# Gate norms of a streaming encoder layer: the sums as a row from one product with ones, and the row's powers on GpSimd in four pieces

## The reference, cut to what matters

```python
def rmsnorm(x, g):
    x32 = x.astype(jnp.float32)
    y = x32 * lax.rsqrt(jnp.mean(x32 * x32, axis=-1, keepdims=True) + EPS)
    return (y * g.astype(jnp.float32)).astype(x.dtype)
...
    h = h + mix @ w_out
    gate = jax.nn.sigmoid((rmsnorm(h, g_ple) @ w_pg).astype(jnp.float32))
    h = h + (gate * (p_i @ w_ple).astype(jnp.float32)).astype(h.dtype)
```

## Time and profile before

| | us |
|---|---|
| three timed runs: median (lowest to highest) | 2471.99 (2470.08 to 2472.39) |
| the profiled execution's own time | 2471.64 |
| its span, first to last instruction | 2469.8 |

### The profile page before, as it was taken

One profiled execution on the slowest core, in us unless ns is written; L12 is line 12 of the kernel. 1 busy time (PEld: TensorE's weight loads), 2 busy tenths in 40 slices (PEclk: granted clock), 3 DMA queues, 4 the chain that ended last, 5 costly groups with the idle time before them and its releaser, 6 DMA issues.

```text
span 2469.8 us, 27263 instructions
## 1 busy us (share of the span) xinstructions
PE 2446.9 (99%) x11188; PEld 2012.1 (81%) x11188; DVE 1036.0 (42%) x1584; ACT 641.5 (26%) x1005; POOL 217.7 (9%) x329
## 2 busy tenths in 40 slices
PE   9999999999999999999999999999999999999997
PEld 7888888888887888888888788888888888888886
DVE  5443343443445234444543433434434542344444
ACT  6221221221232223322432122122122232232223
POOL 1101101101101000000010110110110100000001
PEclk9999999999999999999999999999999999999998
DMA  6343243343243333223242432432432433322322
GB/s 213 107 127 117 83 122 116 88 121 118 87 121 120 99 98 107 70 79 114 80 150 85 134 107 81 138 107 77 139 111 77 129 117 118 110 72 86 94 68 103
DMA packets 180396, 264.84 MB, mean 107 GB/s; under 512 B 16720, under 2 KB 128656, under 8 KB 178992
## 3 DMA queue, kind: packets, MB, share of 16 engines
q1 hardware_dynamic: 143040, 171.87, 23.0%
q0 software_dynamic: 23376, 77.79, 9.8%
q10 hardware_dynamic: 13856, 13.44, 2.3%
HBM read 226.02 MB, written 37.02 MB: 106 GB/s over the span
## 4 chain that ended last, share of the span: by engine, by line
PE 97%; DVE 2%; DMA 0%; issue 0%; ACT 0%; POOL 0%; DVEq 0%; SPq 0%; ACTq 0%; POOLq 0%
PE acc L1360 88%; PE side L1360 8%; PE osb L1586 1%; PE side L1436 0%; PE side L1549 0%; PE side L1489 0%; DMA raw<-in_w_in 0%; DVE st L1071 0%; DVE Sp L1087 0%; DVE Ss L1095 0%; DVE HT L1340 0%; DMA Z<-in_x_t 0%; PE osb L1360 0%; DVE Z L1250 0%; DVE HT L1239 0%
## 5 line engine op out<-in xcount | busy, mean ns | idle before, releaser
L1360 PE MATMUL acc<-Ahi,Whi 128*128 128x512 f32 x2048 | 812.0, 396 | 7.2 <-DVE Alo L850 4.0
L1360 PE MATMUL acc<-Alo,Whi 128*128 128x512 f32 x2048 | 799.1, 390 | 0.0
L1360 PE MATMUL acc<-Ahi,Wlo 128*128 128x512 f32 x2048 | 798.9, 390 | 0.0
L485 ACT ACTIVATE Whi<-raw 128x1024 fp32r<-128x1024 f32 x319 | 337.9, 1059 | 1479.0 <-PE acc L1360 1465.7
L846 DVE TENSOR_TENSOR Wlo<-raw,Whi 128x1024 fp32r<-128x1024 f32 x319 | 390.8, 1225 | 733.7 <-ACT Whi L485 733.3
L1360 PEld LDWEIGHTS acc<-Ahi,Whi 128*128 128x128 f32 x2048 | 385.4, 188 | 90.7 <-issue 10.7
L1360 PE MATMUL acc<-Whi,Ahi 128*128 128x512 f32 x1152 | 452.3, 393 | 0.0
L1360 PEld LDWEIGHTS acc<-Alo,Whi 128*128 128x128 f32 x2048 | 385.2, 188 | 81.7
L1360 PEld LDWEIGHTS acc<-Ahi,Wlo 128*128 128x128 f32 x2048 | 385.7, 188 | 79.6 <-issue 1.0
L1360 PE MATMUL acc<-Whi,Alo 128*128 128x512 f32 x1152 | 448.9, 390 | 0.0
L1360 PE MATMUL acc<-Wlo,Ahi 128*128 128x512 f32 x1152 | 448.2, 389 | 0.0
(11 more groups left out here) (196 smaller groups left out, 1401.0 us busy)
## 6 DMA issues: line engine op xcount, KB each, us to landing
raw<-in_w_in SPq DMA_DIRECT2D x384, 256.0 KB, 3.0
raw<-in_w_out SPq DMA_DIRECT2D x128, 256.0 KB, 3.2
raw<-in_w_pg SPq DMA_DIRECT2D x128, 256.0 KB, 3.2
Ss<-in_state_ret POOLq DMA_DIRECT2D x64, 256.0 KB, 5.1
out_new_ret_sample<-Ss POOLq DMA_DIRECT2D x64, 256.0 KB, 3.0
kv_parts<-stage ACTq DMA_DIRECT2D x16, 256.0 KB, 2.4
Z<-in_x_t POOLq DMA_DIRECT2D x4, 1024.0 KB, 5.6
Ss<-in_w_ple POOLq DMA_DIRECT2D x8, 512.0 KB, 5.2
```

The lines of the kernel that those rows point to most:

```text
L485: nc.scalar.activation(Whi[:, p % 2], raw[:, p % 2], ACT.Copy).then_inc(w_hi, 1)
L1360: return nc.tensor.matmul(out, lhsT, rhs, start=start, stop=stop)
```

## The change

Only the two gate norms (nn odd) change.

- PE `sums`: one matmul of ones (128 x 128) by `sqacc` (128 x 512) in place of four one-column matmuls. Its result is the row of sums on all partitions.
- DVE `mean_square`: instead of copying four columns it forms sum / 2048 + EPS for the whole 128 x 512 row out of PSUM into `rstd_row`; the two small additions for the sample stay, and `ms` is formed for the sample's column alone.
- POOL: instead of one power of 128 x 5, one of 128 x 1 for the sample and four of 128 x 128 on `rstd_row`, in place; `rstd_done` is raised after the last.
- `diagonals`, `rows` and `rstd_rows`, and the side unit `row`, are gone for these norms.
- DVE waits for `rstd_done` in `gate_ple(0)`, ahead of the first `scaled`.

```diff
@@ side_units @@
-        u += [("sum", 2 * l + 1), ("ple", l, 0, 0), ("row", 2 * l + 1)] + [("ple", l, 0, i) for i in range(1, NT)]
+        u += [("sum", 2 * l + 1)] + [("ple", l, 0, i) for i in range(NT)]
@@ gpsimd @@
-                rsqrt(2 * l + 2)
+
+                po.wait_ge(side_free, freed("sum", 2 * l + 1))
+                po.wait_ge(ms_done, 2 * l + 2)
+                settle(po)
+                nc.gpsimd.tensor_tensor(rstd[:, NPT:NT], ms[:, NPT:NT], mhalf[:, NPT:NT], ALU.pow)
+                for t in range(NPT):
+                    cols = slice(t * P, (t + 1) * P)
+                    last = nc.gpsimd.tensor_tensor(rstd_row[:, cols], rstd_row[:, cols],
+                                                   mhalf[:, 0:1].to_broadcast([P, P]), ALU.pow)
+                last.then_inc(rstd_done, 1)
                 for g in range(1, G_OUT):
                     po.wait_ge(wple_low, l * G_OUT + g)
@@ vector, mean_square @@
-                evac(("sum", nn), copy(msum[:, 0:NPT]))
+                if nn % 2:
+                    evac(("sum", nn), lambda bank: nc.vector.tensor_scalar(
+                        rstd_row[:], bank, 1.0 / D, EPS, ALU.mult, ALU.add))
+                else:
+                    evac(("sum", nn), copy(msum[:, 0:NPT]))
...
-                nc.vector.tensor_scalar(ms[:], msum[:], 1.0 / D, EPS, ALU.mult, ALU.add).then_inc(ms_done, 1)
+                cols = slice(NPT, NT) if nn % 2 else slice(0, NT)
+                nc.vector.tensor_scalar(ms[:, cols], msum[:, cols], 1.0 / D, EPS, ALU.mult, ALU.add).then_inc(ms_done, 1)
@@ vector, gate_ple @@
                         ve.wait_ge(ssq_done, (2 * l + 2) * G_OUT)
+                        ve.wait_ge(rstd_done, 2 * l + 2)
@@ vector, pg_jobs @@
                     if s == 9:
                         ple(0, 0)
-                        diagonals(2 * l + 1)
-                    if s == 10:
-                        rstd_rows(2 * l + 1)
@@ tensor, sums @@
-                for t in range(NPT):
-                    last = mm(bank[:, t:t + 1], sqacc[:, t * P:(t + 1) * P], ones[:, 0:1])
+                if nn % 2:
+
+                    last = mm(bank, ones[:], sqacc)
+                else:
+                    for t in range(NPT):
+                        last = mm(bank[:, t:t + 1], sqacc[:, t * P:(t + 1) * P], ones[:, 0:1])
@@ tensor, rows @@
-                pe.wait_ge(diag_done, nn + 1)
+                pe.wait_ge(diag_done, nn // 2 + 1)
@@ tensor, pg_jobs @@
-                    if s == 10:
-                        rows(2 * l + 1)
```

## The result

The changed kernel takes 2586.17 us (median of four, 2584.96 to 2587.42) against 2471.76 us for the kernel before; the ratio is 1.0463 (95% interval 1.0451 to 1.0476). It is slower by 114.4 us, 57.2 us a layer on average. The forecast was 2593 us with a range of 2545 to 2635.

The account below looks back on a forecast made before the run. PE bounds the kernel, busy 99% of the span. Each layer's factors come 62.0 us later, less 1.7 slack, plus 0.2 clock: 60.5 us; 2471.64 + 2 x 60.5 = 2592.6, so 2593 us, range 2545 to 2635 (8 in 10).

Parts of the forecast that it names:

- The deciding term: POOL's powers: 160.5 ns a column plus 0.388 us, so 20.9 us a 128-column piece, 83.7 us for four a layer.
- PE slack of 1.7 us: Between emptying the sample's acc tile and its first matmul in the next stream: 1.71 us, taken off the 62.0 us delay.
- start of POOL: Powers begin on POOL at 1014.9 us, after the new product and DVE's longer first step.
- The first rival: A POOL power is cheap on a long row, under 43 ns a column: all hidden, 2469.7 us; chance 11%.
- 4X - 23.5: Loss of a layer in us when one 128-column power on POOL takes X us; nothing lost below X = 5.9.
- the clock: After its wait PE resumes at half speed for 3.4 us, costing 1.7; mostly covered, so 0.2 us added a layer.
- what POOL does to DVE: POOL powers block DVE's Wlo subtractions; three Wlo between pieces lengthen the powers' chain by 3.2 us a layer.
- the turns: POOL and DVE alternate instruction by instruction, the blocked one waiting for the whole other; 3 x 1.07 = 3.2 us.
- list of signs: Expected in the profile: four powers near 20.9 us a layer, six Wlo of 19 to 22, PE stalls of 11, 11, 33.
- The fourth rival: POOL's power does not shut DVE out: a layer loses 3.2 us less, 2586 us; inside the forecast's range, no separate chance.
- PE's gain: One product costing 0.89 us replaces work at the gate norm: 0.95 us saved a layer, 1.9 us in two.
- The queue behind the powers: POOL's next w_ple load stands behind the powers, landing 6.0 us after them; costs at most a few tenths.

Follow-up runs that it names:

- other forms of the power: The changed kernel with a full exponent tile in layer 0, one 512-column power in layer 1, an extra 128 x 4 power in both: 2585.86 us.
- one piece: The changed kernel with only one of the four 128 x 128 powers a layer, the rest of the row left as mean squares: 2470.16 us, ratio 0.9992.
- no POOL: The changed kernel with the row's square root on ACT and reciprocal on DVE, POOL keeping only the sample's column: 2470.67 us, ratio 0.9995.
- The unread powers: The kernel before plus four 128 x 128 powers a layer that nobody reads, ahead of the w_ple loads in POOL's queue: 2575.82 us against 2471.27.
- the two pieces: The changed kernel with two of the four 128 x 128 powers a layer, half of the row left as mean squares: 2504.25 us.

## Why the prediction was right, and where its steps failed

**The deciding term was right.** A piece was put at 20.9 us from two short rows, 1 and 5 columns; it takes 20.7, and the line holds to 512 columns. With the PE slack of 1.7 us and the start of POOL (forecast 1014.9; measured 1016.02, less the 1.16 us by which this execution was already late at the product with ones, 1013.64 against 1012.48 in the earlier trace rows: 1014.86) this gives the loss to within a few us. The first rival, a power that streams on a long row, falls with the 81.9 us of one 512-column instruction. The figure of the Trainium skill named beside it does not carry over to the power: the GPSIMD Engine Reference (section 3.1) gives about 2.6 cycles at 1.2 GHz for an element of a two-input instruction, an estimated 2.2 ns; products here take 2.0 to 2.5 ns a column (1040 and 1293 ns for 512), powers 159.4. One small slip: the general form of the sum, 4X - 23.5, leaves out the 0.2 us of the clock (with X = 20.93 it gives 60.2, not 60.5).

**The step that failed is what POOL does to DVE.** It took the turns of the earlier trace rows, seen between a POOL product and DVE, for a property of any POOL instruction with two operands, and put 3.2 us a layer into the chain and three PE stalls of 11, 11 and 33 us into the list of signs. There is one stall of 55.1 us, and every `Wlo` beside a power takes 1.22. The fourth rival, "POOL's power does not shut DVE out", is what happened, at its price: 2586 us forecast, 2586.17 measured. That the two agree so closely is in part luck: the price holds the two errors below, and these in part cancel. I had folded it into the forecast's range; the rows on which I put the turns above it were rows of products, and the one row of a power showed only the power giving way. The Trainium skill (SBUF — State Buffer, "SBUF: two separate sides") says of a DVE instruction with two SBUF inputs and a GpSimd instruction that reads SBUF that whichever starts first gets the port pair they share for the whole instruction, and the other is blocked; the products agree, the powers don't: they wait for a DVE instruction that is running, but don't hold one up. Why was not settled; operand stride and length are excluded.

**Two sizes were off.** The piece was put 0.22 us too long, 0.9 us a layer. The clock was put at 0.2 us, from a slow stretch of 3.4 us that the freeing of the tiles would cover. In layer 0 PE was slow for nearly 6 us instead (0.50 from 1100.9 to 1105.3, 1.00 only from 1106.6) and never waited for a tile after the first. The scaling began 59.14 us late against the earlier trace rows, the sample tile's product 58.0 us late against the earlier trace rows, the next step (1106.59, before 1048.33 in the kernel's time line) 58.26: of the 1.71 us of slack 0.83 went to the clock. In layer 1 it was 0.34 (scaling 2373.82 against 2257.52, next step 2380.36 against 2265.43: 116.30 and 114.93 us late, so 1.37 of the slack was left). That the tiles cover a shorter stretch was right: in layer 0 of the version with other forms of the power the clock was up after 3 us, PE did wait for the sample's tile, and the 15 matmuls from 1101.16 to 1106.69 took 5.53 us instead of 6.20, so that the clock cost 0.16 us there (0.83 - 0.67). The windows, then the wait:

```profile
1101.20:1103.80 2.60, 2.60 (x6) 2.08 (x7) 2.40 (x4) 1.65 (x3) 0.00 (x0) 0.50 0.67 202
1104.20:1107.00 2.80, 2.44 (x11) 1.61 (x10) 2.44 (x5) 2.45 (x4) 0.00 (x0) 1.00 0.03 9
```

```profile
1105.89 0.50 PE L1379 MATMUL acc<-Whi,Ahi 128*128 128x512 f32 x1 [0.36 <-ACT stage L568]
```

What sets the length of the slow stretch stays open. The turns and both errors make 3.2 + 0.9 - 0.6 = 3.5 us in layer 0 and 3.2 + 0.9 - 0.1 = 4.0 in layer 1, 7.5 in all. The profiled execution took 2586.62 us, 6.0 less than the 2592.6 forecast, and was already 1.16 us late ahead of the norm: 7.1 to be accounted for.

**PE's gain** of 0.95 us a layer is in the rows as worked out, 0.89 for the new product. In the change it lies ahead of a wait and only lengthens it. The medians of the two versions without the stall lie 1.6 us (one piece) and 1.1 us (no POOL) below the kernel before, but both intervals of the ratio hold 1: in time the gain is not established.

**The queue behind the powers** was rightly put at a few tenths here, because the factors and the `w_ple` block come late together: ACT's split of the block began at 1105.91, right behind its `Whi` copy, without a wait. The unread powers show that it is a second price of nearly the same size, 104.6 us by itself. From the two times, a change that left the powers ahead of the load and only dropped the wait for the factors would win an estimated 10 of the 114 us; it was not run.

## What to carry to other kernels

A row of per-token factors on all partitions repeats the same 512 numbers 128 times; with a fast operation that is cheap, with one of 159 ns a column it turns 5 columns (1.2 us) into 512 (83 us). Before moving work to an engine that looks idle, divide the time between the inputs and the date at which the result is due by the count of columns, and read the cost of a column from two sizes of that very operation, not of its neighbours. Look also at what stands behind the new work in that engine's queue: a long instruction that nobody waits for still delays every DMA behind it.

## What the runs showed of the hardware that was not expected

- A power on GpSimd costs 0.3 to 0.4 us plus 159.4 ns a column from 1 to 512 columns, whether the exponent is a full tile (20.85 us for 128 columns) or one column at stride 0 (20.7), in one instruction or in four.
- DVE's two-input subtraction runs at full speed beside a power (1.22 us), but not beside a product (1.58 and 1.93 us); a power that starts while such a DVE instruction runs is later by up to 1.0 us.
- A product with a stride-0 second operand took 1040 ns for 512 columns, one whose second operand steps through a row of 128 four times 1293. Its own row was addressed as 4 x 128 too, so that the stride is the reason is not shown.
- A reciprocal of 128 x 512 on DVE took 3.35 us, five times a copy.
- After the 55 us stalls of the change PE ran its first matmuls at the lower clock (0.50) for 5.8 us in layer 0 and 4.5 us in layer 1; after 57 us in layer 0 of the version with other forms of the power for 3 us; after the 13.7 us stalls of the two pieces for some 5 us. The length of the slow stretch does not follow the length of the stall. After 47 us of idleness and one more wait of 1.0 us in between, it was about 9 us.
